# A two-layer hybrid decoder step: prompt memory in quarters between the mixers' products, the SSD norm behind the GLA chunks, and two more output tiles in halves

## The chip, the cores and the metric

One core of a Trainium2 chip. The metric is the device time of one execution in microseconds, the median of three runs for the kernel before. All data is fp32, so each matrix product appears in the trace as two MATMUL instructions.

## The reference

One inference step for a prompt group (256 tokens) and a sample group (8 sequences of 8 tokens) through two layers of width 1024. 320 token columns are processed together. Cut to what matters here:

```python
xn = rms_norm(x, norm_mix)
h = xn @ w_in                                     # split among the three mixers
o_mla = mla_attend(...)                           # 8 heads; samples over 16 cached pages of 128 tokens each
o_ssd = ssd_mixer(...)                            # Mamba-2 chunk scan, 4 heads, old state h0, then norm per group
o_gla = gla_mixer(...)                            # gated linear attention, chunks of 64, old state S0, then norm
x = x + concat([o_mla, o_ssd, o_gla]) @ w_o
x = x + mem_attend(rms_norm(x, norm_mem), mk, mv) # prompt: mk, mv from mem_prompt (256 tokens); samples: cached
x = x + conv_ffn(rms_norm(x, norm_ffn))

def mem_kv(mem, lp):
    k = rms_norm((mem @ mem_wk).reshape(b, n, MEM_HEADS, MEM_HEAD_DIM), mem_k_norm)
    v = (mem @ mem_wv).reshape(b, n, MEM_HEADS, MEM_HEAD_DIM)
```

The updated states of SSD and GLA, the latents, mk and mv are outputs too.

## The kernel before, in words

Activations lie with their features on the 128 partitions: x is 8 key tiles of 320 columns (256 prompt columns TP, then 64 sample columns). Each engine has its own program, written out by hand in the order in which it runs; they meet in semaphores. A PSUM bank is taken from a named ring (`proj`: banks 0 to 2, `score`: 3 and 4, `mix`: 5 to 7) by `banks.open`, filled by TensorE (`banks.full`), and given back by the engine that empties it; the next opener waits for that (`banks.before`).

Per layer, TensorE's program is: 18 tiles of the input projection with the latent attention's inputs between them; `memory_keys(l, 0)`; `prompt_attention`; `tokens_first` (transposes of values and convolved inputs to tokens); `gla_decay`; `ssd`; `gla_inputs`; `ssd_norm`; `gla`; `gla_norm`; `cache` (the samples' attention over 128 pages, 32 groups of four); `mixed_out`; `memory`; `mlp`.

**Prompt memory.** `memory_keys(l, part, some)` makes a tile of 128x256: parts 0 and 1 are the two key tiles mk, 2 and 3 the two value tiles mv, 4 the sum of squares of mk. `some` is the range of key tiles k of this call, and a tile may be spread over calls. Before, parts 1 to 3 run in halves of four key tiles (L1015) in the attention's iterations h = 1 to 6. ScalarE copies the finished tiles in its own attention loop, at h = 2, 4, 6 and 7 (L2152 and the copies at L1863).

**SSD.** TensorE's `ssd` makes cumulative sums (L695, L696, L706), decays (L713), C·B products (L719), the chunk states h1 and h2 (L729 to L736), then for each group g the interaction with old states `yi` (L745, and sixteen narrow products at L748, which read hT, the old SSD state transposed) and the products `y` (L759). VectorE puts Y together (L1453 to L1466), ScalarE squares it, TensorE sums the squares (`y_ss`, L778), ScalarE makes the factor of it (L1868, L1871), and VectorE's `ssd_out` (L1472) writes mix tiles 4 and 5. ScalarE in `ssd` also scales the old state in its natural layout, hnat, in sixteen copies (L1863, after a wait for hnat_in), and only then empties GLA's key transposes (`kwt`) in five copies, also L1863 (`gla_keys`).

**GLA.** `gla_inputs` transposes keys (L794, L795) and makes the scores (L800). TensorE's `gla` begins with a wait for `kwt` to be emptied, then runs four chunks c: state increments (L810), a product for the new SSD state (`ssd_states`, L769), outputs (L821, L824); then the samples (L833, L838), the samples' state (L847), the last `ssd_states`, and in `gla_norm` the sums of squares (`o_ss`, L858). The cache's first product (L877) follows.

**Output projection.** For tiles m = 0 to 2 (`EARLY` = 3) the prompt's columns are done during the end of `cache` (`mixed_out_prompt`, L969). `mixed_out` then waits for the last sample's attention, makes `ov_new` (L977, L978), and runs eight tiles at L992: m = 0 to 2 over the 64 sample columns only, m = 3 to 7 over all 320. Each has eight key tiles, in `MIX_ORDER` (4, 5, 6, 7, 0, 1, 2, 3). VectorE adds each tile to x in `residual` (L1625), in the order of m.

**Weights and states.** Weights come through a ring of seven slots of 512 KB, in the order of `SLOTS`, on SyncE's DMA queue. `fill` (L2460) waits, slot by slot, until the last reader of what the slot held has signalled: for the two tiles of memory input and the two of wv that reader is value tile 1 (`"mv", l, 1`). Around the mixers SyncE's program is in this order:

```python
sp.dma_start(hT_t, io["ssd_t"][l]).then_inc(hT_in, 16)        # L2500
limit[:] = [filled[0] + NSLOT]
fill(("wuv", "wo"))                                           # L2460: wuv, then wo tiles 0 to 5
...
sp.dma_start(hnat_t, io["ssd_n"][l]).then_inc(hnat_in, 16)    # L2506
...
sp.dma_start(gsb_t, io["gla"][l]).then_inc(gsb_in, 16)        # L2509
for t in range(2):
    group(l, t)                                               # L2468, L2479: cache pages
sp.wait_ge(*on["mix_gla"].at(l, 1))
```

Slots that wo tiles 0 and 1 take held the memory input, tiles 2 and 3 take wk's, and 4 and 5 take wv's.

Of the kernel before, what the change touches and what calls it, by code (L numbers as in the profile page):

```python
# [27 lines left out]
ACT = mybir.ActivationFunctionType  # L28
# [178 lines left out]
def trunk(nc, io):  # L207
    ctx = ExitStack()
    with ctx:
# [285 lines left out]
        def _(pe):  # L495
# [151 lines left out]
            def prompt_attention(l):  # L647
                for h in range(HEADS + 3):
                    if h < HEADS:
                        prompt_scores(l, h)  # L650
                    if 1 <= h <= 6:
                        memory_keys(l, (h + 1) // 2, range(0, 4) if h % 2 else range(4, KD))
                    if h == 7:
                        memory_keys(l, 4)
                    if 0 <= h - 2 < HEADS:
                        prompt_values(l, h - 2)
                    if h >= 3:
                        prompt_out(l, h - 3)

            def gates(l):  # L660
# [7 lines left out]
                last.then_inc(banks.full("gate", l), 1)  # L668

            def tokens_first(l):  # L670

                for f in (4, 5):
                    b = banks.open("mix", "tok", l, f)
                    pe.wait_ge(*banks.before("tok", l, f))
                    for i in range(2):
                        pe.transpose(b[:, i * P:(i + 1) * P], gv[:, f - 4, i * P:(i + 1) * P], cc("ident"))
                    pe.transpose(b[0:TS, 2 * P:3 * P], gv[:, f - 4, TP:T], cc("ident")).then_inc(banks.full("tok", l, f), 1)
                pe.wait_ge(*on["xu_ready"].at(l))
                for f in range(4):
                    b = banks.open("mix", "tok", l, f)  # L680
                    pe.wait_ge(*banks.before("tok", l, f))
                    for i in range(2):
                        pe.transpose(b[:, i * P:(i + 1) * P], xu[:, f, i * P:(i + 1) * P], cc("ident"))
                    pe.transpose(b[0:TS, 2 * P:3 * P], xu[:, f, TP:T], cc("ident")).then_inc(banks.full("tok", l, f), 1)
# [4 lines left out]
            def ssd(l):  # L689
# [51 lines left out]
                pe.wait_ge(hT_in, 16 * (l + 1))  # L741
                for g in range(2):
                    b = banks.open("mix", "yi", l, g)
                    pe.wait_ge(*banks.before("yi", l, g))
                    mm(b[:, P:TP], h1[:, g, :], xu[:, 4 + g, P:TP], **F)  # L745
                    for s in range(NB):
                        at = TP + NQ * s
                        last = mm(b[:, at:at + NQ], hT[:, g, s, :], xu[:, 4 + g, at:at + NQ], **F)  # L748
                    last.then_inc(banks.full("yi", l, g), 1)
                for g in range(2):  # L750
                    b = banks.open("mix", "y", l, g)
                    pe.wait_ge(*banks.before("y", l, g))
                    for i in range(3):
                        n = P if i < 2 else TS
                        pe.wait_ge(*banks.emptied("G", l, i))
                        pe.wait_ge(*on["xdt_ready"].at(l))
                        for hh in range(2):
                            h = 2 * g + hh
                            last = mm(b[64 * hh:64 * hh + 64, i * P:i * P + n], tok[0:n, i, h * 64:h * 64 + 64],  # L759
                                      dec[0:n, i, h, 0:n], **F)  # L760
                    last.then_inc(banks.full("y", l, g), 1)
# [40 lines left out]
            def gla(l):  # L802
# [32 lines left out]
                for s in range(NB):  # L835
                    for hh in range(2):
                        out = b[64 * hh:64 * hh + 64, 0:P].rearrange("p (g t) -> p g t", g=2)[:, :, NQ * s:NQ * s + NQ]
                        last = mm(out, gsb[:, s, :], qtm[:, hh::2, TP + NQ * s:TP + NQ * s + NQ],  # L838
                                  start=False, stop=(s == NB - 1))
                last.then_inc(banks.full("o", l, 4), 1)  # L840
                pe.wait_ge(*on["vm_ready"].at(l))
                for half in range(2):
# [9 lines left out]
            def gla_norm(l):  # L852

                pe.wait_ge(*on["o_sq"].at(l))
                for g in range(2):
                    b = banks.open("mix", "o_ss", l, g)
                    pe.wait_ge(*banks.before("o_ss", l, g))
                    mm(b[:, 0:T], cc("blk64"), sq[:, g, :], **F).then_inc(banks.full("o_ss", l, g), 1)  # L858

# [111 lines left out]
            def mixed_out(l):  # L971

                pe.wait_ge(*banks.emptied("po", l, NB - 1))
                b = banks.open("mix", "ov_new", l)
# [5 lines left out]
                last.then_inc(banks.full("ov_new", l), 1)  # L980
                for m in range(KD):
                    split = m < EARLY
                    if split:
                        w, b, at = early[m], banks.of("wo", l, m), TP
                    else:
                        w, at = slot("wo", m, "wo", l, m).rearrange("p (k c) -> p k c", k=KD), 0
                        b = banks.open("proj", "wo", l, m)
                        pe.wait_ge(*banks.before("wo", l, m))
                    for k in MIX_ORDER:
                        if m == 0 and k == 0:  # L990
                            pe.wait_ge(*banks.emptied("ov_new", l))
                        last = mm(b[:, at:T], w[:, k, :], mix[:, k, at:T], start=(k == MIX_ORDER[0]), stop=(k == MIX_ORDER[-1]))  # L992
                    last.then_inc(banks.full("wo", l, m), 1)

            mem_slots = []
# [192 lines left out]
            for l in range(DEPTH):  # L1188
# [25 lines left out]
                gla_inputs(l)  # L1214
                ssd_norm(l)
                gla(l)
# [8 lines left out]
        def _(dve):  # L1225
# [283 lines left out]
            def gla(l):  # L1509
                for c in range(4):  # L1510
# [11 lines left out]
                    dve.wait_ge(*V.last)  # L1522
                ssd_out(l)
                dve.wait_ge(gsb_in, 16 * (l + 1))
                TTO(gso, gsb, ge[:, TP + NQ - 1:T:NQ].unsqueeze(2).broadcast_to([P, NB, 64]), ALU.mult).then_inc(V.step(), 1)
                dve.wait_ge(*V.last)
                for half in range(2):
# [3 lines left out]
                    TTO(o, o, b[:, 0:256].rearrange("p (b v) -> p b v", b=4), ALU.add).then_inc(V.free("dSs", l, half), 1)  # L1531
                states(l, 1, 1)
                dve.wait_ge(*on["o_rs"].at(l))
                for g in range(2):
# [322 lines left out]
        def _(act):  # L1857
# [129 lines left out]
            def prompt_attention(l):  # L1987
                scale = QK ** -0.5
                for h in range(HEADS + 3):
# [14 lines left out]
                    if h == 2:  # L2004
                        zg_sigmoid(l, 1)
                    if h in (2, 4, 6, 7):
                        memory_keys(l, (h + 1) // 2)

# [14 lines left out]
            def ssd(l):  # L2023
# [4 lines left out]
                for k in range(4):  # L2028
                    token_tile(l, k)
                gla_decay(l)  # L2030
                act.wait_ge(*on["cs_diff"].at(l))
# [12 lines left out]
                act.wait_ge(*on["g_diff"].at(l))  # L2044
                exp(gek, gek, scale=1.0 / 16).then_inc(A.fire(on["gek_ready"]), 1)
                own_samples(l, bm, 256, "bm_ready")
                act.wait_ge(hnat_in, 16 * (l + 1))
# [7 lines left out]
                f(sq[:, 0:2, :], ysb, ACT.Square).then_inc(A.fire(on["y_sq"]), 1)  # L2055
                for g in range(2):
                    b = banks.of("y_ss", l, g)
                    act.wait_ge(*banks.filled("y_ss", l, g))
                    ln(ytmp[:, g, :], b[:, 0:T], 128).then_inc(A.free("y_ss", l, g), 1)
                act.wait_ge(*A.last)  # L2060
                exp(ytmp, ytmp, scale=-0.5).then_inc(A.fire(on["y_rs"]), 1)

# [16 lines left out]
            def gla(l):  # L2079
# [4 lines left out]
                act.wait_ge(*A.last)  # L2084
                f(sq[:, 0:2, :], osb, ACT.Square).then_inc(A.fire(on["o_sq"]), 1)
                for g in range(2):
# [651 lines left out]
```

## Time and profile before

| | |
|---|---|
| runs, median (lowest to highest) | 1406.98 us (1404.48 to 1411.47) |
| profiled execution, its own time | 1413.27 us |
| its span, first to last instruction | 1411.5 us |
| mean granted TensorE clock | 0.976 of full speed |
| TensorE busy | 1375.7 us (97%) |
| TensorE weight load busy | 1131.1 us (80%) |
| VectorE, ScalarE, GpSimd busy | 894.0, 594.0, 206.0 us |
| DMA | 175.24 MB, mean 124 GB/s |

Shares of busy time are averages over stages. Matmuls are pipelined, so a busy TensorE isn't one at its peak, and a product takes twice as long when the granted clock is 0.50 as when it is 1.00. An instruction's line can be that of a helper: L1863 is every ScalarE copy, L1871 every exponential.

### The profile page before, as it was taken

To read this page: it belongs to the slowest core of one execution; us is meant where nothing else is said; L and a number is where in the kernel's file an instruction comes from. 1 tells how busy PE (TensorE), PEld (TensorE's weight loads), DVE (VectorE), ACT (ScalarE), POOL (GpSimd) and SP (SyncE) were. 2 spreads that over 40 slices of the span, in tenths; PEclk is the share of its full clock that TensorE was granted. 3 is DMA by queue.
4 is the path that set the end of the run, shared out by engine and by line. 5 is a ranking of instruction groups with operands and counts; after the bars stand their busy time and mean duration, and the time that the engine had idled before them with its cause. 6 is when DMAs were issued, how large, how long until landed. Compare 5 with 4: busy or idle time off the path is not lost.

```text
span 1411.5 us, 23318 instructions
## 1 busy us (share of the span) xinstructions
PE 1375.7 (97%) x8148; PEld 1131.1 (80%) x8148; DVE 894.0 (63%) x1850; ACT 594.0 (42%) x1607; POOL 206.0 (15%) x330
## 2 busy tenths in 40 slices
PE   8999899999998999999999999999999999999999
PEld 6676767777775899999976677677778669999999
DVE  1337658888325878797423565688882258878964
ACT  2166647767215333320012766577761253333200
POOL 1001112221011222220000101211200121222200
PEclk9999989999989999999999998999998999999999
DMA  7331434443034344444433323444421353444442
GB/s 272 111 121 60 168 104 130 124 112 96 21 128 170 120 150 134 136 136 144 141 133 123 106 93 121 129 129 114 123 69 60 105 185 120 150 127 143 132 137 88
DMA packets 79718, 175.24 MB, mean 124 GB/s; under 512 B 11793, under 2 KB 46130, under 8 KB 78706
## 3 DMA queue, kind: packets, MB, share of 16 engines
q1 hardware_dynamic: 75952, 164.11, 36.5%
q0 software_dynamic: 3360, 9.18, 2.1%
q8 instruction: 66, 1.08, 0.3%
q14 instruction: 50, 0.41, 0.1%
q10 hardware_dynamic: 290, 0.45, 0.1%
HBM read 167.42 MB, written 6.29 MB: 123 GB/s over the span
## 4 chain that ended last, share of the span: by engine, by line
PE 62%; DVE 25%; ACT 9%; issue 3%; DMA 1%; SPq 1%; DVEq 0%
PE pair L517 13%; PE pair L877 8%; DVE area L1675 8%; PE pair L878 8%; PE pair L1149 8%; PE pair L992 5%; ACT area L1871 4%; PE bank L1149 3%; PE bank L913 2%; DVE area L1693 2%; DVE area L1699 2%; PE pair L884 2%; ACT area L1877 2%; PE pair L969 2%; DVE area L1691 2%
## 5 line engine op out<-in xcount | busy, mean ns | idle before, releaser
L517 PE MATMUL pair<-xg,slot 128*128 128x320 f32 x768 | 212.2, 434 | 3.0 <-DMA slot<-in_weights 2.2
L1544 DVE TENSOR_REDUCE small<-sq 128x8 f32<-128x512 f32 x256 | 168.1, 682 | 47.2 <-ACT sq L2110 45.4
L517 PEld LDWEIGHTS pair<-xg,slot 128*128 128x128 f32 x768 | 144.9, 190 | 65.9 <-issue 2.9
L2110 ACT ACTIVATE sq<-pair 128x512 f32<-128x512 f32 x256 | 152.3, 595 | 5.8 <-DVE small L1544 5.8
L1675 DVE TENSOR_TENSOR area<-slot 128x512 f32<-128x512 f32 (+1 forms) x128 | 85.4, 668 | 42.7 <-PE pair L1149 42.7
L1118 PE MATMUL pair<-sq,area 128*128 128x160 f32 x736 | 112.1, 301 | 0.1
L877 PE MATMUL pair<-wkq,area 128*128 128x288 f32 x320 | 107.6, 418 | 0.0
L1118 PEld LDWEIGHTS pair<-sq,area 128*128 128x128 f32 x736 | 102.8, 190 | 1.9 <-DVE area L1675 1.2
L878 PE MATMUL pair<-wkq,area 128*128 128x288 f32 x320 | 103.8, 406 | 0.0
L1871 ACT ACTIVATE area<-area 128x336 f32<-128x336 f32 (+6 forms) x114 | 62.1, 549 | 94.1 <-DVE area L1693 79.9
L2315 POOL DMA_INDIRECT krT<-in_cache_r,kr_rows x64 | 61.2, 956 | 223.8 <-PE pair L884 221.4
L1863 ACT ACTIVATE xg<-pair 128x64 f32<-128x64 f32 x256 | 56.1, 219 | 84.0 <-PE pair L878 53.2
L2223 ACT ACTIVATE area<-area,par 128x336 f32<-128x336 f32 x44 | 29.4, 668 | 142.3 <-DVE area L1716 141.1
L1863 ACT ACTIVATE area<-pair 128x160 f32<-128x160 f32 (+6 forms) x156 | 45.2, 309 | 97.4 <-PE pair L1149 91.6
L1863 ACT ACTIVATE area<-bank 128x160 f32<-128x160 f32 (+8 forms) x112 | 39.4, 364 | 85.5 <-PE bank L1149 57.6
L1118 PE MATMUL pair<-olat,slot 128*128 128x160 f32 x480 | 75.0, 299 | 0.0
L878 PEld LDWEIGHTS pair<-wkq,area 128*128 128x128 f32 x320 | 60.8, 190 | 16.8
L877 PEld LDWEIGHTS pair<-wkq,area 128*128 128x128 f32 x320 | 56.2, 190 | 17.6 <-issue 1.4
L1118 PEld LDWEIGHTS pair<-olat,slot 128*128 128x128 f32 x480 | 68.6, 190 | 0.3
L2307 POOL TENSOR_SCALAR xg<-x,par 128x320 f32<-128x320 f32 x24 | 29.4, 1227 | 261.5 <-DVE x L1625 181.1
L992 PE MATMUL pair<-mix,slot 128*128 128x320 f32 (+1 forms) x256 | 67.4, 443 | 0.0
L877 PE MATMUL pair<-wkq,kept 128*128 128x288 f32 x192 | 65.5, 423 | 0.4 <-DMA kept<-in_cache 0.2
(456 smaller groups left out, 2700.9 us busy)
## 6 DMA issues: line engine op xcount, KB each, us to landing
slot<-in_weights SPq DMA_DIRECT2D x216, 512.0 KB, 3.6
area<-in_cache SPq DMA_DIRECT2D x160, 130.0 KB, 2.1
kept<-in_cache SPq DMA_DIRECT2D x96, 130.0 KB, 2.2
slot<-in_weights SPq DMA_DIRECT2D x18, 384.0 KB, 3.6
xg<-in_ssd_t SPq DMA_DIRECT2D x2, 1024.0 KB, 4.7
area<-in_ssd_n SPq DMA_DIRECT2D x2, 1024.0 KB, 11.6
hs_out<-area POOLq DMA_DIRECT2D x2, 1024.0 KB
x<-in_x SPq DMA_DIRECT2D x4, 320.0 KB, 6.4
```

What stands on the lines that cost most here:

```text
L517: last = mm(out[:, 0:T], w[:, k, :], xg[:, k, :], start=(k == 0), stop=(k == KD - 1))
L877: mm(pair[:, 0:288], page, wkq[:, 0:4, at:at + 72], **F)
L878: last = mm(pair[:, 512:800], page, wkq[:, 4:8, at:at + 72], **F)
L992: last = mm(b[:, at:T], w[:, k, :], mix[:, k, at:T], start=(k == MIX_ORDER[0]), stop=(k == MIX_ORDER[-1]))
L1118: last = mm(out[:, 0:HALF], held[:, k, :], moving[:, k, :], start=(k == 0), stop=(k == 3))
L1149: last = mm(out[:, 0:HALF], held[:, k, :], moving[:, at + k, :], start=(b == 0 and k == 0), stop=(b == 2 and k == n - 1))
L1544: dve.tensor_reduce(ssk[:, t % 2, 8 * j:8 * j + 8], ksq[k % 3], AX.X, ALU.add).then_inc(V.fire(on["k_summed"]), 1)
L1675: TTO(w[k], a, b, op).then_inc(V.fire(on["w_sum"]), 1)
L1863: return f(out, in_, ACT.Copy, **kw)
L1871: return f(out, in_, ACT.Exp, **kw)
L2110: f(ksq[k % 3].rearrange("p (a h) d -> p a h d", a=2), b4[:, :, :, NQ - at:NQ - at + 64], ACT.Square).then_inc(A.fire(on["key_free"]), 1)
L2315: pool.indirect_dma_start(out=krT[n % KR_GROUPS][:, :], out_offset=None, in_=io["cache_r"].rearrange("l a c t -> (l a c) t"), in_offset=ba ...
```

## The change

TensorE's prompt attention keeps parts 1 (in quarters, h = 1 to 4), 4 and half of part 2; the rest of part 2 goes among the token transposes, and part 3 in two halves around the second `yi` group. ScalarE's copies of these tiles move along. `ssd_norm` goes from ahead of `gla` to behind the samples' outputs in it; ScalarE's factor for Y goes behind the GLA outputs, with GLA's squares in other tiles of sq; VectorE's `ssd_out` goes behind the last state. In the output projection, tiles 3 and 4 are made in halves of four key tiles, and the order of tiles is changed. SyncE's and GpSimd's programs are not edited.

```diff
@@ -648,10 +648,12 @@
                         prompt_scores(l, h)
-                    if 1 <= h <= 6:
-                        memory_keys(l, (h + 1) // 2, range(0, 4) if h % 2 else range(4, KD))
+                    if 1 <= h <= 4:
+                        memory_keys(l, 1, quarter(h - 1))
                     if h == 7:
                         memory_keys(l, 4)
+                    if h in (8, 9):
+                        memory_keys(l, 2, quarter(h - 8))
                     if 0 <= h - 2 < HEADS:
@@ -666,6 +668,9 @@
                 last.then_inc(banks.full("gate", l), 1)
+
+            def quarter(i):
+                return range(2 * i, 2 * i + 2)
@@ -677,6 +682,8 @@
                 for f in range(4):
+                    if f >= 2:
+                        memory_keys(l, 2, quarter(f))
                     b = banks.open("mix", "tok", l, f)
@@ -740,6 +747,8 @@
                 for g in range(2):
+                    if g:
+                        memory_keys(l, 3, range(0, 4))
                     b = banks.open("mix", "yi", l, g)
@@ -747,6 +756,7 @@
                     last.then_inc(banks.full("yi", l, g), 1)
+                memory_keys(l, 3, range(4, KD))
                 for g in range(2):
@@ -838,6 +848,7 @@
                 last.then_inc(banks.full("o", l, 4), 1)
+                ssd_norm(l)
                 pe.wait_ge(*on["vm_ready"].at(l))
@@ -855,7 +866,7 @@
                     pe.wait_ge(*banks.before("o_ss", l, g))
-                    mm(b[:, 0:T], cc("blk64"), sq[:, g, :], **F).then_inc(banks.full("o_ss", l, g), 1)
+                    mm(b[:, 0:T], cc("blk64"), sq[:, 2 + g, :], **F).then_inc(banks.full("o_ss", l, g), 1)
@@ -970,6 +981,7 @@
+                first_half(l, 3)
                 pe.wait_ge(*banks.emptied("po", l, NB - 1))
@@ -978,19 +990,28 @@
                 last.then_inc(banks.full("ov_new", l), 1)
-                for m in range(KD):
-                    split = m < EARLY
-                    if split:
-                        w, b, at = early[m], banks.of("wo", l, m), TP
+                first_half(l, 4)
+                for m in (0, 3, 1, 4, 2, 5, 6, 7):
+                    split, half = m < EARLY, m in (3, 4)
+                    if split or half:
+                        w, b, at = early[m], banks.of("wo", l, m), TP if split else 0
                     else:
...
                         pe.wait_ge(*banks.before("wo", l, m))
-                    for k in MIX_ORDER:
+                    for k in MIX_ORDER[4:] if half else MIX_ORDER:
                         if m == 0 and k == 0:
...
                     last.then_inc(banks.full("wo", l, m), 1)
+
+            def first_half(l, m):
+
+                early[m] = slot("wo", m, "wo", l, m).rearrange("p (k c) -> p k c", k=KD)
+                b = banks.open("score", "wo", l, m)
+                pe.wait_ge(*banks.before("wo", l, m))
+                for k in MIX_ORDER[:4]:
+                    mm(b[:, 0:T], early[m][:, k, :], mix[:, k, :], start=(k == MIX_ORDER[0]), stop=False)
@@ -1212,7 +1233,6 @@
                 gla_inputs(l)
-                ssd_norm(l)
                 gla(l)
@@ -1520,7 +1540,6 @@
                     dve.wait_ge(*V.last)
-                ssd_out(l)
                 dve.wait_ge(gsb_in, 16 * (l + 1))
@@ -1530,6 +1549,7 @@
                 states(l, 1, 1)
+                ssd_out(l)
                 dve.wait_ge(*on["o_rs"].at(l))
@@ -2003,8 +2023,10 @@
                         zg_sigmoid(l, 1)
-                    if h in (2, 4, 6, 7):
-                        memory_keys(l, (h + 1) // 2)
+                    if h == 5:
+                        memory_keys(l, 1)
+                    if h == 8:
+                        memory_keys(l, 4)
@@ -2027,6 +2049,7 @@
                     token_tile(l, k)
+                memory_keys(l, 2)
                 gla_decay(l)
@@ -2043,6 +2066,7 @@
                 exp(gek, gek, scale=1.0 / 16).then_inc(A.fire(on["gek_ready"]), 1)
+                memory_keys(l, 3)
                 own_samples(l, bm, 256, "bm_ready")
@@ -2053,12 +2077,6 @@
                 f(sq[:, 0:2, :], ysb, ACT.Square).then_inc(A.fire(on["y_sq"]), 1)
-                for g in range(2):
-                    b = banks.of("y_ss", l, g)
-                    act.wait_ge(*banks.filled("y_ss", l, g))
-                    ln(ytmp[:, g, :], b[:, 0:T], 128).then_inc(A.free("y_ss", l, g), 1)
-                act.wait_ge(*A.last)
-                exp(ytmp, ytmp, scale=-0.5).then_inc(A.fire(on["y_rs"]), 1)
@@ -2082,7 +2100,13 @@
                 act.wait_ge(*A.last)
-                f(sq[:, 0:2, :], osb, ACT.Square).then_inc(A.fire(on["o_sq"]), 1)
+                f(sq[:, 2:4, :], osb, ACT.Square).then_inc(A.fire(on["o_sq"]), 1)
+                for g in range(2):
+                    b = banks.of("y_ss", l, g)
+                    act.wait_ge(*banks.filled("y_ss", l, g))
+                    ln(ytmp[:, g, :], b[:, 0:T], 128).then_inc(A.free("y_ss", l, g), 1)
+                act.wait_ge(*A.last)
+                exp(ytmp, ytmp, scale=-0.5).then_inc(A.fire(on["y_rs"]), 1)
                 for g in range(2):
```

## Rows read from the trace of the kernel before

**Rows 1.** The page: busy time of TensorE, and engines' shares of the last chain.

```profile
PE 1375.7 (97%) x8148; PEld 1131.1 (80%) x8148; DVE 894.0 (63%) x1850; ACT 594.0 (42%) x1607; POOL 206.0 (15%) x330
...
PE 62%; DVE 25%; ACT 9%; issue 3%; DMA 1%; SPq 1%; DVEq 0%
```

**Rows 2.** Windows: stretch: length, busy by engine (instructions), PEclk, DMA share, GB/s.

```profile
120.00:150.00 30.00, 27.12 (x140) 21.65 (x140) 20.79 (x63) 21.46 (x65) 2.10 (x2) 1.00 0.23 84
150.00:167.00 17.00, 15.14 (x128) 13.86 (x126) 9.60 (x26) 11.48 (x33) 0.00 (x0) 1.00 0.50 189
167.00:178.00 11.00, 10.05 (x64) 6.24 (x64) 7.20 (x14) 7.68 (x25) 4.50 (x5) 0.69 0.12 36
178.00:194.00 16.00, 16.00 (x137) 8.36 (x134) 6.17 (x13) 3.61 (x10) 1.69 (x3) 0.61 0.09 36
...
849.00:866.00 17.00, 15.14 (x100) 13.89 (x98) 7.33 (x18) 8.36 (x27) 0.00 (x0) 0.80 0.47 175
...
363.00:380.00 17.00, 16.70 (x127) 14.23 (x127) 2.74 (x7) 1.67 (x3) 0.00 (x0) 1.00 0.00 1
380.00:396.00 16.00, 15.13 (x70) 14.09 (x71) 2.65 (x6) 2.24 (x5) 2.35 (x2) 0.59 0.40 131
```

**Rows 3.** Timeline of SyncE's queue: start us, length us, instruction; both layers.

```profile
145.12 0.47 SPq L2506 DMA_DIRECT2D area<-in_ssd_n  x1
...
844.06 0.48 SPq L2506 DMA_DIRECT2D area<-in_ssd_n  x1
```

**Rows 4.** Waits of SyncE's queue, 110 to 200 us: in total, times, longest.

```profile
SPq L2460 <- PE pair L1015: 26.4, 1, 26.4
```

**Rows 5.** DMA of the SSD state: issue to landing in layer 0, and both layers.

```profile
area<-in_ssd_n SPq DMA_DIRECT2D x1, 1024.0 KB, 12.1
...
DMA to landing us min/median/max: 11.0/11.6/12.1
```

**Rows 6.** Timeline of TensorE, layer 0: start us, us, instruction, [idle before].

```profile
140.32 1.89 PE L1015 MATMUL pair<-slot 128*128 128x256 f32 x8
...
166.38 2.14 PE L748 MATMUL bank<-mix,xg 128*128 128x8 f32 x16
...
176.23 1.34 PE L778 MATMUL bank<-sq,const 128*128 128x320 f32 x4
177.51 0.32 PE L810 MATMUL pair<-area,kept 128*32 128x64 f32 x8
...
182.36 0.44 PE L810 MATMUL pair<-area,kept 128*32 128x64 f32 x8
...
185.78 0.69 PE L833 MATMUL bank<-area 64*64 64x64 f32 x8
...
193.56 1.17 PE L877 MATMUL pair<-wkq,kept 128*128 128x288 f32 x2
```

**Rows 7.** Timeline of ScalarE, layer 0.

```profile
133.53 0.36 ACT L2152 ACTIVATE sq<-pair 128x256 f32<-128x256 f32 x1
...
167.03 4.76 ACT L1863 ACTIVATE area<-area 128x128 f32<-128x128 f32 x16
173.33 1.45 ACT L1863 ACTIVATE kept<-pair 64x128 f32<-64x128 f32 x5 [1.54 <-PE pair L795]
```

**Rows 8.** Timeline of TensorE, layer 1.

```profile
839.01 1.89 PE L1015 MATMUL pair<-slot 128*128 128x256 f32 x8
...
868.32 1.85 PE L748 MATMUL bank<-mix,xg 128*128 128x8 f32 x16
...
879.87 0.32 PE L810 MATMUL pair<-area,kept 128*32 128x64 f32 x8
...
892.70 1.17 PE L877 MATMUL pair<-wkq,kept 128*128 128x288 f32 x2
```

**Rows 9.** Timeline of TensorE, layer 0, output projection.

```profile
380.87 0.43 PE L977 MATMUL bank<-olat,slot 128*128 128x64 f32 x2 [0.98 <-DVE olat L1586]
```

## The prediction

> **What bounds the kernel now.** The page comes first: TensorE is busy 97% of the span and carries 62% of the chain that ended last [rows 1], so the two questions are where it works at half clock and where it has nothing to do. The windows by stage answer both [rows 2]. The prompt attention (120 to 150 us) has 2.9 us of gaps at full clock; the state space mixer's start has 1.9 us; from 167 to 178 the granted clock is 0.69 and from 178 to 194 it is 0.61; the output projection's start, 380 to 396, has 0.59. The two levels are 1.2 and 2.4 GHz, so 0.59 over 16 us means 13.1 us at 1.2 GHz. Layer 1 repeats the pattern some 699 us later. These are the places that the change fills with dense matmuls. The third view is SyncE's queue with its waits and landings [rows 3, 4, 5]. The weight slots of the output projection are reloaded into the slots of the memory input, and those count as read when the second tile of prompt memory values is full. SyncE waited 26.4 us for that, at L2460, and only behind those six loads does it issue the natural-layout SSD state (145.12), the GLA state and the first pages.
>
> **The change, part by part, against the profiled execution** (1413.27 us; its span is 1411.5). That execution is 6.3 us above the median of 1406.98; a difference from it carries over to the median.
>
> *Memory quarters out of the attention.* Four key tiles of matmuls take 1.73 us (1.89 with the tail, [rows 6]). The attention loses three such halves, 5.2 us of TensorE, and keeps three. Per head it is then ScalarE's and VectorE's chain that sets the pace. What ScalarE saves on it is the key tile's square and copy between two heads' exponentials, 133.53 to 134.06 [rows 7], 0.53 us, and that at h = 7 a little less stands ahead of the last heads; I take 0.6 (ends 0 and 1.2). The two quarters among the token transposes fit into the 1.9 us of gaps of 150 to 167 [rows 2]: nothing, and if that cover were gone, 0.85 us each.
>
> *Memory halves around the interactions with the old state.* Two halves, 3.5 us, now stand before and behind the second group (L748), whose last matmul ended at 166.38 + 2.14 = 168.5 [rows 6]. So the second value tile is full at 168.5 + 3.5 - 0.6 = 171.4, and at about 170.9 if the denser stretch also keeps the clock up through L748. It was full at 140.32 + 1.89 = 142.2. In layer 1 the old end is 870.2. That layer lies 3.2 us further behind layer 0 there than at its start, after the stretch 849 to 866 at clock 0.80 [rows 2, 8]; the quarters should keep that clock up, which gives 870.2 + 3.5 - 0.6 - 3.2 = 869.9, against 840.9 before.
>
> *What is queued behind that.* SyncE waits for this tile before six slot loads (3 MB) and then 1 MB of SSD state. From tile full to state landed took 145.12 + 12.1 - 142.2 = 15.0 us in layer 0 and 844.06 + 11.0 - 840.9 = 14.2 us in layer 1 [rows 3, 5, 6, 8]. ScalarE used that state at 167.03, 9.8 us after it landed; this cover is gone. It now lands at 170.9 + 15.0 = 185.9 and at 869.9 + 14.2 = 884.1. ScalarE reaches the wait early (it now also waits for the value tile, and copies the samples' B rows in 1.7 us), scales the state in 4.76 us and copies the GLA key tiles in 1.45 us [rows 7], and without those TensorE may not start the GLA chunks (L810). They start at 192.1 and 890.3 where they started at 177.51 and 879.87: 14.6 and 10.4 us later. In the meantime TensorE has its Y products and GLA scores and then nothing, for about 13 us. The y_ss product (1.34 us with its tail) goes from ahead of the chunks to behind them; all that work, and VectorE's, lies in the wait.
>
> *From the chunks to the cache.* It took 193.56 - 177.51 = 16.05 us in layer 0, mostly at 1.2 GHz, and 892.70 - 879.87 = 12.83 us in layer 1, mostly at 2.4 [rows 6, 8]. Now y_ss comes on top. Upper bound, all at 1.2 GHz: 1.0 for the first chunk, three turns like 182.36 to 185.78 (10.3), 7.8 for the rest (to 193.56), twice y_ss's 1.07 (2.1): 21.2. Lower bound, clock as in layer 1: 12.83 + 1.3 = 14.1. Behind a long gap the nearest row is layer 0's second half, where this same mix stayed at the low level once there; I take 20 in both layers: +3.9 and +7.2. Sum for the mixers: 14.6 + 3.9 + 10.4 + 7.2 = **+36.1 us**. ssd_out's two instructions on VectorE (1.0 us) go to where it idled 3 us for ScalarE: nothing.
>
> *Output projection.* A dense first half of tile 3 (four key tiles of 320 columns, 2.1 us) covers the 0.98 us that TensorE waited at 380.87 [rows 9]; tile 4's covers ScalarE's copy; the second halves stand between the narrow passes. Dense halves of 2.1 us then alternate with 1.8 us of narrow ones. At 363 to 380 [rows 2], 3.7 us dense against 2.1 us narrower, the clock was 1.00. If it stays up here too, 13.1 us at half clock become 6.5. I count 6.6 + 1.0 = 7.6 per layer, **-15.2 us**; lower bound 2 (the gaps alone). The slots of tiles 3 and 4 are of the early batch; the later tiles' slots (wuv's and tile 0's) are freed within about 2 us of before and read over 12 us later: nothing. No DMA is added. VectorE's residual takes tiles in their old order and gets tile 1 later than tile 3; the last tile is still last: nothing.
>
> Sum: 36.1 - 15.2 = +20.9, so 1434 for the profiled execution and **1427 us** for the median.
>
> Two rules of the Trainium skill weigh on this. The trace first: the state landed 15.0 and 14.2 us after the release, its 4.2 MB sharing with some 1.3 MB of pages and GLA state behind it. "DMA: Bandwidth & Descriptors" (Bandwidth) gives 425 GB/s for large transfers, by which 4.2 MB would be an estimated 10 us, and the sum about 10 us lower. The second is among the rivals.
>
> **The rivals.**
> A, *the memory release doesn't hold the state back*. It ends faster. The place is SyncE's order, the price the 25 us of late chunk starts. If the state landed within 2 us of the release, the chunks would start about where they did: 1407 - 15.2 for the projection - 3.2 for layer 1's stretch + 2 for the Y products behind the memory halves, some 1390. It decides at the landing: with 20 us from chunks to cache the change breaks even at about 4 us from release to landing, with 14 at about 10. The wait row, with its releaser L1015, speaks against it [rows 4], and so do both landings. 5%.
> B, *short wait and warm chunks*: the transfer needs only what its own 4.2 MB take at the 390 GB/s or so of the old burst (11 us), and the GLA chunks climb to full clock as in layer 1: -7.2 -11.8 from my sum, 1408. Between it and the forecast lie the cases where one of the two holds. For it: layer 1's chunks ran warm. Against: they came straight from 4 us of dense scores, these come from nothing. 14%.
> C, *the projection stays at half clock*: half of the mixture is still narrow; only the gaps are won, +13.2, so 1440. Against: 363 to 380. 12%.
> D, *the attention goes cold*: rid of three dense halves, its heads keep a third of transposes. In layer 1, 849 to 866 fell to 0.80 right behind a run of transposes and gaps, and lost 3.2 us. The same in each attention gives +6.4 to the value tile and all behind it: 1433. "TensorE: Matmul & The Clock Gate" (Part 4) says that transposes don't count as work for the clock; by that rule the attention would fall in both layers, and the trace agrees as far as layer 1. 11%.
> E, *the edit doesn't do what it says*: y_ss and the quarters change nothing by themselves. It ends in one of the above.
>
> **How the numbers follow.** Forecast 58%, A 5%, B 14%, C 12%, D 11%. The range takes B's upper part, D and C: 1412 to 1441. A measurement can tell about 0.5%, 7 us. Faster by more than that: A, 5%. Within it, 1400 to 1414: B's lower half and the lowest end of the forecast, 9%. Slower: 86%.
>
> **What would show it.** SyncE's wait at L2460 grows from 26 to 55 us; ScalarE has a wait of some 13 us before its sixteen state copies, TensorE one of about the same before L810; DMA is busy at 171 to 186, not 142 to 158. The chunks run at clock 0.5 to 0.7. The projection's first 16 us show a clock near 1.0 and no gap ahead of L977. I am wrong if the copies start at 167 to 173 as before, or if the release is signalled from inside the attention.

## The result and the profile after

The changed kernel takes 1440.08 us (median of 4 executions, 1438.1 to 1443.02) beside 1405.73 us for the kernel before. The ratio is 1.022, with a 95% interval of 1.0177 to 1.0263: slower by 25 to 37 us. Forecast were 1427 us and a range of 1412 to 1441. The profiled execution took 1438.1 us, which is 24.8 us more than that of before (1413.27); the sum in the prediction was made against that one and gave 20.9.

The windows of the kernel after, by stage (columns as in [rows 2], which they answer to). The third to fifth are the wait, the chunks of layer 0 and the projection; the last three lie in layer 1:

```profile
120.00:150.00 30.00, 24.89 (x118) 18.30 (x117) 20.79 (x63) 20.86 (x64) 2.10 (x2) 0.94 0.00 1
150.00:167.00 17.00, 16.76 (x131) 15.19 (x131) 10.12 (x26) 9.69 (x29) 0.00 (x0) 1.00 0.01 2
178.00:194.00 16.00, 2.81 (x26) 1.41 (x26) 0.50 (x2) 6.93 (x23) 0.00 (x0) 0.59 0.62 232
194.00:212.00 18.00, 18.00 (x122) 8.93 (x122) 5.50 (x11) 3.77 (x9) 1.61 (x3) 0.50 0.05 17
...
404.00:428.00 24.00, 24.00 (x119) 18.51 (x118) 6.02 (x13) 4.64 (x10) 5.60 (x5) 1.00 0.52 174
...
862.00:879.00 17.00, 16.76 (x131) 15.19 (x131) 9.91 (x26) 9.69 (x29) 0.00 (x0) 1.00 0.01 3
...
890.00:903.00 13.00, 0.00 (x0) 0.00 (x0) 0.00 (x0) 5.85 (x21) 0.00 (x0) 0.53 0.77 290
903.00:925.00 22.00, 21.77 (x149) 10.97 (x150) 6.19 (x13) 5.29 (x13) 1.70 (x3) 0.50 0.05 20
```

The reader sees three things. The stretch behind the attention, which fell to 0.80 in layer 1 before, is at 1.00 in both layers. The projection, at 0.59 before, is at 1.00. Between them TensorE does nothing at all for 13 us (no instruction from 890 to 903, while DMA runs at 290 GB/s), and all the work from the chunks to the cache then runs at 0.50, the lower of the clock's two levels.

Why it stands still is told by SyncE's queue in the kernel after: its wait between 110 and 200 us, the issues in layer 0, and (DMA view, 140 to 220 us) the landing of the state there. They answer to [rows 3 to 5]:

```profile
SPq L2484 <- PE pair L1036: 55.9, 1, 55.9
```

```profile
171.30 2.84 SPq L2484 DMA_DIRECT2D slot<-in_weights  x6
174.23 0.44 SPq L2530 DMA_DIRECT2D area<-in_ssd_n  x1
```

```profile
area<-in_ssd_n SPq DMA_DIRECT2D x1, 1024.0 KB, 10.8
```

The wait for the second value tile (L1036 is the old L1015) has grown from 26.4 to 55.9 us; the state that stood at 145.12 in the queue is issued at 174.23. On the other side ScalarE, layer 0, answers to [rows 7]:

```profile
171.30 0.38 ACT L1883 ACTIVATE mv<-pair 128x256 f32<-128x256 f32 x1 [6.44 <-PE pair L1036]
171.72 1.71 ACT L1883 ACTIVATE area<-area,const 64x256 f32<-64x256 f32 x4
185.02 4.78 ACT L1883 ACTIVATE area<-area 128x128 f32<-128x128 f32 x16 [11.59 <-DMA area<-in_ssd_n]
189.70 1.44 ACT L1883 ACTIVATE kept<-pair 64x128 f32<-64x128 f32 x5
```

And TensorE, layer 0 and then the first chunk and the cache of layer 1, to [rows 6, 8, 9]; L820 is the chunks' first product (old L810), L888 the cache's (old L877), L1014 a first half of tiles 3 and 4:

```profile
169.29 1.97 PE L1036 MATMUL pair<-slot 128*128 128x256 f32 x8
...
191.19 0.44 PE L820 MATMUL pair<-area,kept 128*32 128x64 f32 x8 [15.46 <-ACT kept L1883]
...
212.68 1.17 PE L888 MATMUL pair<-wkq,kept 128*128 128x288 f32 x2
...
398.68 2.37 PE L1014 MATMUL pair<-mix,slot 128*128 128x320 f32 x8
...
427.42 4.47 PE L517 MATMUL pair<-xg,slot 128*128 128x320 f32 x16
...
903.23 0.44 PE L820 MATMUL pair<-area,kept 128*32 128x64 f32 x8 [15.28 <-ACT kept L1883]
...
924.71 1.17 PE L888 MATMUL pair<-wkq,kept 128*128 128x288 f32 x2
```

The row at 427.42 is the memory stage's first product. In the kernel before it stood here (TensorE, layer 0):

```profile
416.23 4.47 PE L517 MATMUL pair<-xg,slot 128*128 128x320 f32 x16
```

Taken from these rows and their old counterparts, the 24.8 us are:

| where | layer 0 | layer 1 |
|---|---|---|
| chunks start later | +13.7 | +10.4 |
| chunks to cache | 21.5 instead of 16.05: +5.4 | 21.5 instead of 12.8: +8.7 |
| from the cache's start to the memory's first product behind the projection | -7.9 | -7.1 |

That is 38.2 - 15.0; the remaining 1.6 lies between the layers, where layer 1's attention starts 13.0 us later than before and layer 0's memory stage 11.2. There the 64 us from the memory's first product on ran at a granted clock of 0.97, against 1.00 before; why isn't known. (In the table, 13.0 is taken off the times of layer 1.)

### The profile page after: what moved, and what is told of

The parts are those of the page before. It is cut to its first block, busy times and chain, and to the rows that moved or that the text cites. A ratio compares the mean times of both kernels' runs of the same rounds, so it can differ in the third digit from the quotient of the medians.

```text
span 1436.3 us, 23318 instructions
## 1 busy us (share of the span) xinstructions
PE 1372.7 (96%) x8148; PEld 1121.1 (78%) x8148; DVE 892.7 (62%) x1850; ACT 594.9 (41%) x1607; POOL 207.0 (14%) x330
## 4 chain that ended last, share of the span: by engine, by line
PE 62%; DVE 23%; ACT 9%; issue 3%; DMA 2%; SPq 1%; DVEq 0%
PE pair L517 12%; PE pair L888 9%; PE pair L889 8%; DVE area L1695 8%; PE pair L1170 7%; ACT area L1891 4%; PE pair L1005 3%; PE bank L1170 2%; PE bank L924 2%; DVE area L1713 2%; ACT area L1883 2%; PE pair L895 2%; DVE area L1719 2%; ACT area L1897 2%; PE pair L980 2%
## 5 line engine op out<-in xcount | busy, mean ns | idle before, releaser
L888 PE MATMUL pair<-wkq,area 128*128 128x288 f32 x320 | 107.6, 418 | 0.0
L1883 ACT ACTIVATE area<-pair 128x160 f32<-128x160 f32 (+8 forms) x154 | 44.8, 309 | 98.2 <-PE pair L1170 91.6
L888 PEld LDWEIGHTS pair<-wkq,area 128*128 128x128 f32 x320 | 56.2, 190 | 17.6 <-ACT sq L2134 1.4
L888 PE MATMUL pair<-wkq,kept 128*128 128x288 f32 x192 | 66.1, 426 | 0.0
L889 PE MATMUL pair<-wkq,kept 128*128 128x288 f32 x192 | 63.6, 414 | 0.0
```

Source lines behind the costliest of these rows:

```text
L888: mm(pair[:, 0:288], page, wkq[:, 0:4, at:at + 72], **F)
L889: last = mm(pair[:, 512:800], page, wkq[:, 4:8, at:at + 72], **F)
L1883: return f(out, in_, ACT.Copy, **kw)
```

## The experiments

Two theories. **The release**: everything that was lost comes from SyncE's order, in which the state stands behind the slots that the second value tile frees. The rival, **the mixture**: the matmuls moved in among the mixers, or the sum of squares behind the chunks, cost time by themselves, on TensorE's path or through its clock. The third question, apart from both, is what the projection gives. Ratios are to the kernel before, on the same chip in the same series, with the 95% interval.

**The changed kernel, with the states issued first.**

```diff
                 sp.dma_start(hT_t, io["ssd_t"][l]).then_inc(hT_in, 16)
-                limit[:] = [filled[0] + NSLOT]
-                fill(("wuv", "wo"))
-                limit.clear()
...
                 for t in range(2):
                     group(l, t)
+                limit[:] = [filled[0] + NSLOT]
+                fill(("wuv", "wo"))
+                limit.clear()
```

The fill now stands behind the loads of both states and the first two groups of pages. Expected:

> The changed kernel, with SyncE issuing the natural-layout SSD state, the GLA state and the first eight pages ahead of the seven weight slots. Theory (the whole loss is the state that lands 14 to 15 us after a release that now comes 29 us later): ScalarE's sixteen copies start right behind the samples' B rows, at about 173.4 us in layer 0, the GLA chunks at about 179.5 instead of 191.2, and the chunks take 16 to 18 us instead of 21.5. That is some 16 us less per layer, and about 22 us less in each with the clock's share at best: 1390 to 1405 us, below the kernel before by up to 1%. Rival (the memory halves between the products with the old state and the norm behind the chunks cost by themselves, by their time and their clock): the chunks start earlier but the time stays at 1420 us or more, ratio above 1.01.

Measured: 1415.09 us, ratio 1.004 (1.0017 to 1.0062), 12 executions. Most of the loss is gone, yet it falls short of what the release theory expected. The state was issued at 115.1 us and took this long to land (DMA view, 110 to 190 us):

```profile
area<-in_ssd_n SPq DMA_DIRECT2D x1, 1024.0 KB, 6.8
```

So it was there at 122, and still the chunks began late. ScalarE and TensorE in layer 0 of this run, and the windows from the chunks to the cache in both layers:

```profile
171.41 0.38 ACT L1883 ACTIVATE mv<-pair 128x256 f32<-128x256 f32 x1 [6.44 <-PE pair L1036]
171.83 1.71 ACT L1883 ACTIVATE area<-area,const 64x256 f32<-64x256 f32 x4
173.44 4.77 ACT L1883 ACTIVATE area<-area 128x128 f32<-128x128 f32 x16
178.11 1.44 ACT L1883 ACTIVATE kept<-pair 64x128 f32<-64x128 f32 x5
```

```profile
179.60 0.32 PE L820 MATMUL pair<-area,kept 128*32 128x64 f32 x8 [3.75 <-ACT kept L1883]
```

```profile
179.00:201.00 22.00, 21.40 (x150) 10.78 (x151) 6.18 (x13) 6.07 (x14) 1.70 (x3) 0.54 0.19 74
878.00:900.00 22.00, 21.37 (x148) 10.69 (x149) 6.18 (x13) 5.61 (x13) 1.70 (x3) 0.50 0.15 59
```

A second wait had been hidden behind the first. The change put the copy of value tile 1 ahead of the state's scaling in ScalarE's program; it waits 6.44 us for TensorE, and the GLA key copies, for which the chunks wait, come 3.75 us too late. Behind a gap of 3.75 us the chunks run at half clock, in layer 1 from their first product on as behind a gap of 15.5. In layer 0 they begin at full clock (their first row takes 0.32 us, against 0.44) and fall within the first 4 us.

**The kernel before, with the states issued first.** The same edit of SyncE's order, and nothing else.

> The kernel before, with the same new order on SyncE. Theory: the state was there 9.8 us before its use and the output projection's weights are read 200 us later, so nothing moves: ratio 0.997 to 1.003. Rival (the burst of weights and states itself slowed something in the attention, so that any new order gains): 5 us or more below the kernel before, and then the first run restores nothing.

Measured: 1406.37 us, ratio 0.9985 (0.9957 to 1.0013). Nothing: in the kernel before the state's landing was hidden, as [rows 7] against [rows 3, 5] say.

**The kernel before, with the release made late.** No matmul is moved; SyncE just waits, ahead of the fill, for the products that now stand beside the second value tile.

```diff
+                sp.wait_ge(*banks.filled("yi", l, 1))
                 limit[:] = [filled[0] + NSLOT]
                 fill(("wuv", "wo"))
```

> The kernel before, TensorE, ScalarE and VectorE as they were; SyncE alone also waits, before the seven slot loads, for the second group of products with the old state (full at 168.5 us in layer 0, 870.2 in layer 1). Theory: the state lands about 14 us after that, at 182.5, the GLA chunks start at about 188.8 instead of 177.5 and take 19 instead of 16 us; in layer 1 10 us later and 6 longer. Together 28 to 32 us: 1434 to 1438 us, though not one matmul has moved. Rival (the loss is in the moved matmuls): 1403 to 1409 us.

Measured: 1444.54 us, ratio 1.0239 (1.0174 to 1.0303). Timeline of SyncE's queue, ScalarE and TensorE of this run, layer 0, and its chunks in layer 1 (L778 is `y_ss`, L810 the chunks' first product, as in [rows 6]):

```profile
168.35 3.32 SPq L2460 DMA_DIRECT2D slot<-in_weights  x7
171.78 0.67 SPq L2507 DMA_DIRECT2D area<-in_ssd_n  x1
...
184.61 4.78 ACT L1863 ACTIVATE area<-area 128x128 f32<-128x128 f32 x16 [17.72 <-DMA area<-in_ssd_n]
...
191.41 2.50 PE L778 MATMUL bank<-sq,const 128*128 128x320 f32 x4 [15.38 <-ACT sq L2055]
```

```profile
909.00:928.00 19.00, 19.00 (x145) 9.51 (x145) 6.27 (x13) 3.80 (x9) 1.70 (x3) 0.50 0.04 16
```

The wait alone, with the memory's matmuls and the sum of squares where they always were, makes a gap of 15.38 us in layer 0 and 14.55 in layer 1, chunks at a clock of 0.60 and 0.50, and the kernel slower by 25 to 43 us; 1434 to 1438 us had been expected. A loss as large as the changed kernel's net one can thus be made without the mixture. The fair measure is the changed kernel with the old projection, further down (1.0328, its interval from 1.0267): by the ratios the late release makes some 34 of its 46 us, and the two intervals barely overlap. The profiled executions lie closer, 1450.58 us here and 1448.71 there. The release also comes 3 us earlier here (SyncE issues the fill at 168.35, in the changed kernel at 171.30). (Here `y_ss` is what waits, since ScalarE's squares stand behind the state's scaling; in the changed kernel it is the chunks.)

**The kernel before, with the new output projection.** `mixed_out` and `first_half` of the changed kernel, all else as before.

> The kernel before with the new mixed_out alone: first halves of tiles 3 and 4 ahead of and behind the samples' value products, second halves between the narrow passes. Theory: the gap of 1.0 us is covered and the granted clock stays at 1.00 through the narrow passes, 7.6 us per layer: 15.2 us, 1390 to 1392 us, ratio 0.989. Rival (the clock falls all the same when the stretch before it isn't the changed one): only the gaps, 2 us, ratio 0.998.

Measured: 1396.89 us, ratio 0.9909 (0.9873 to 0.9944): a gain of 8 to 18 us, 12.8 in the middle. The time is 5 us above the expected 1390 to 1392; the expected ratio, 0.989, lies in the interval.

**The changed kernel, states first, and ScalarE's copy moved behind the state's scaling.**

```diff
-                memory_keys(l, 3)
                 own_samples(l, bm, 256, "bm_ready")
...
+                memory_keys(l, 3)
                 gla_keys(l)
```

> The run with the states first, and ScalarE's copy of the second value tile moved from ahead of the samples' B rows to behind the sixteen state copies. There ScalarE had waited 6.4 us for that tile (until 171.3), so that GLA's key copies came 3.75 us after TensorE had run dry. Theory (that wait, with the gap and the clock it costs, is what the states-first run still lost): the chunks start at about 176 in layer 0, no gap ahead of them, and take 14 to 15 us; 1385 to 1393 us. Rival (the chunks fall to 1.2 GHz because the norm's dense product no longer stands ahead of them): they start at 176 but take 19 to 21 us, 1396 to 1406 us.

Measured: 1394.94 us, ratio 0.9921 (0.9893 to 0.9949), 2 us above the upper end of what was expected. The gap is gone and with it the half clock. TensorE's chunks of layer 0, and the windows from the chunks to the cache in both layers:

```profile
175.83 0.32 PE L820 MATMUL pair<-area,kept 128*32 128x64 f32 x8
```

```profile
176.00:188.00 12.00, 12.00 (x150) 6.53 (x143) 6.54 (x15) 4.33 (x12) 1.48 (x3) 1.00 0.51 192
864.00:876.00 12.00, 12.00 (x150) 6.41 (x149) 6.53 (x15) 4.32 (x11) 1.16 (x2) 1.00 0.53 198
```

The same 150 matmuls that took 21.5 us take 11.9. What is late next is seen at the cache's ninth pages, TensorE in both layers of this run:

```profile
198.94 0.75 PE L888 MATMUL pair<-wkq,kept 128*128 128x288 f32 x2 [2.27 <-DMA kept<-in_cache]
...
887.66 1.14 PE L888 MATMUL pair<-wkq,kept 128*128 128x288 f32 x2 [2.57 <-DMA kept<-in_cache]
889.55 1.17 PE L888 MATMUL pair<-wkq,kept 128*128 128x288 f32 x2
```

SyncE issues those pages only when the GLA output is done, and the faster chunks reach them sooner. From the cache's first product to the projection's first half it took 187.3 and 189.3 us here, 186.0 and 186.7 in the changed kernel: of the 9.6 us that the chunks gave in each layer, 1.3 and 2.6 went back. Issuing those pages earlier wasn't tried. Such waits aren't a matter of the memory's parts: in the version below that has these back in the attention, with chunks as fast, they are 2.18 and 2.55 us.

**The same, with the sum of squares of Y back ahead of the chunks.** `ssd_norm` between `gla_inputs` and `gla`, its factor and `ssd_out` in their old places.

> The same, and the norm of Y back ahead of the chunks on TensorE, ScalarE and VectorE. Theory of the wait: the norm's place is worth nothing either way, within 4 us of the run before this one. Theory of the norm: the chunks take 13 us again and this one is the faster by 10 to 14 us, 1383 to 1393.

Measured: 1393.41 us, ratio 0.9922 (0.9891 to 0.9954). Its place is worth nothing that can be measured in the time, either way. In the traces the chunks' clock differs: with the sum of squares among them and no gap ahead they were at 1.00 in all four cases (both layers of the run before this one and of the run with the memory's parts back). With it ahead of them and no gap they were at 1.00 from first to last in only two of ten; layer 1 of this run is one that fell, to 0.80 over 13.1 us. Whether its place is the cause wasn't tested by itself.

**The changed kernel, with only ScalarE's copy moved back.** As above, without the change of SyncE's order.

> The changed kernel with ScalarE's copy behind the state copies, SyncE's order untouched. The state lands at 185 whatever ScalarE does before that, so within 4 us of the changed kernel: 1434 to 1444. Rival (ScalarE's wait for the value tile is itself the loss): below 1425.

Measured: 1441.58 us, ratio 1.0252 (1.0194 to 1.031). No gain while the state is late: ScalarE waits at the state instead. This timeline row of its layer 0 shows the longer wait:

```profile
187.97 4.78 ACT L1883 ACTIVATE area<-area 128x128 f32<-128x128 f32 x16 [19.52 <-DMA area<-in_ssd_n]
```

The copy's wait costs something measurable only where the wait for the state is gone.

**The changed kernel, with the old output projection.**

> The changed kernel with the old mixed_out. From the prediction 15 us slower than the changed kernel, from the run with the new projection alone (13 us better than before) 13: 1452 to 1456 us, ratio 1.031 to 1.035. Rival (the projection's gain depends on the rest): 1445 or less.

Measured: 1450.05 us, ratio 1.0328 (1.0267 to 1.0388). The new projection gives some 10 us here by the medians and 15 by the ratios (1.0328 against 1.022), with wide intervals. The mixers' programs are those of the changed kernel, and yet in layer 0 the chunks behind a gap of 15.60 us took 19.4 us and not 21.5, since the clock rose just ahead of the cache. TensorE, layer 0 of this run:

```profile
193.16 0.44 PE L820 MATMUL pair<-area,kept 128*32 128x64 f32 x8 [15.60 <-ACT kept L1873]
...
212.53 0.65 PE L888 MATMUL pair<-wkq,kept 128*128 128x288 f32 x2
```

**The changed kernel, with the memory's matmuls and copies back in the attention.** The direct undo of that part (TensorE's and ScalarE's); SyncE's order, the place of the sum of squares and the projection stay as in the changed kernel.

```diff
-                    if 1 <= h <= 4:
-                        memory_keys(l, 1, quarter(h - 1))
+                    if 1 <= h <= 6:
+                        memory_keys(l, (h + 1) // 2, range(0, 4) if h % 2 else range(4, KD))
...
-                    if h in (8, 9):
-                        memory_keys(l, 2, quarter(h - 8))
...
```

> After, with the prompt memory's matmuls and copies back in the attention as before; the weights' issue, the norm of Y behind the chunks and the new projection stay as in after. The SyncE theory: the slot of value tile 1 is free at about 142 us again, the state is issued by about 146 and lands by about 158, the chunks start at 173 to 178 in layer 0 and the kernel takes 1390 to 1400 us (before, less what the new projection gave by itself, 12.8 us). The rival, by which the norm of Y behind the chunks or its factor in ScalarE's later place costs something of its own once the state is early: chunks to cache over 17 us and a time of 1403 or more.

Measured: 1399.38 us, ratio 0.9929 (0.9902 to 0.9955), at the upper end of what the release theory said. SyncE's queue issues the state where it did before, and TensorE's chunks of layer 0 (now L813) start without a wait. They start at 181.82, not at 173 to 178 as expected; the 17 us from 154.82 on ran at a granted clock of 0.70 here, and the 10 us behind them at 0.52. But the windows from the chunks to the cache, with the sum of squares still among them, are at full clock or nearly so in both layers:

```profile
144.81 0.39 SPq L2519 DMA_DIRECT2D area<-in_ssd_n  x1
```

```profile
181.82 0.32 PE L813 MATMUL pair<-area,kept 128*32 128x64 f32 x8
```

```profile
181.00:194.00 13.00, 13.00 (x153) 6.99 (x153) 6.90 (x15) 4.33 (x11) 1.49 (x3) 0.98 0.03 11
872.00:885.00 13.00, 13.00 (x154) 7.12 (x153) 6.93 (x15) 4.82 (x12) 1.70 (x3) 1.00 0.09 29
```

**The kernel before, with the states first and the new projection.**

> Before, with the states and first pages issued ahead of the weights and the new projection; the memory's matmuls in the attention as in before. If the projection is the whole of the gain, this ties with the version that has the memory's parts in the mixers, the states first and the copy behind them (0.9921): ratio 0.988 to 0.994. If that redistribution has a gain of its own (chunks that ran at full clock throughout there), this one is at 0.995 or more and its chunks show a granted clock under 0.9. If the redistribution cost something of its own (the cache's wait for pages there, 2.3 and 2.6 us, with the stretches at half clock behind it), this one is under 0.988, and its cache groups wait for no page.

Measured: 1401.0 us, ratio 0.9936 (0.9911 to 0.9961). It ties with the version that keeps the memory's parts in the mixers (0.9921). Its window ahead of the chunks of layer 1, and then the same window of the run with states first and the copy moved, where the parts are in the mixers (there it takes in the first 2 us of the chunks):

```profile
850.00:866.00 16.00, 15.76 (x108) 14.91 (x109) 12.29 (x28) 9.36 (x26) 1.37 (x2) 0.71 0.03 10
```

```profile
850.00:866.00 16.00, 15.76 (x127) 11.88 (x127) 12.46 (x28) 11.13 (x32) 4.46 (x5) 1.00 0.36 120
```

The redistribution does keep the clock up (1.00 in the second, 0.71 in the first), as meant. Over all the profiled kernels, the first 16.5 us behind the attention ran at 0.69 to 0.79 in five of twelve cases with the parts in the attention, and at 1.00 in all twelve with the parts in the mixers. Yet the end isn't earlier by anything measurable. The page waits take some of it back, but this version has one too, 2.50 us in layer 0 (none in layer 1), so they account for little of the tie; where the rest went stays open. Of the versions tried none beats the simplest, the kernel before with the new projection alone (0.9909); the four others that have the new projection and an early state (0.9921 to 0.9936) tie with it.

## Why the prediction was right

**The release: right, nearly to the microsecond.** Value tile 1 was full at 169.29 + 1.97 = 171.3 (said: 170.9). In layer 1 the tile was full at 883.5 against a forecast of 869.9 without layer 0's delay, of which 13.0 us had come by then: 870.5. SyncE waited 55.9 us (said: 55), ScalarE 11.59 ahead of the sixteen copies (said: 13). The run with nothing but a late release shows that this wait makes most of such a loss by itself. The runs with states first and the copy moved, and with the memory's parts back in the attention, show that the parts' new place and the sum of squares cost nothing measurable once the state is early. Only ScalarE's copy does (below).

**From tile full to state landed: 13.8 and 13.5 us**, for the 15.0 and 14.2 that I carried over from the kernel before. By the rule of the Trainium skill that I had set beside it, "DMA: Bandwidth & Descriptors" (Bandwidth), the estimate was 10 us; the measured values lie between, nearer to the trace.

**Start of the chunks: +13.7 and +10.4 us** for +14.6 and +10.4. TensorE's gap of 15.46 us was put at 13.

**Chunks to cache: mis-sized.** I took 20 us and kept 21.2 as the upper bound, for all at half clock; both layers took 21.5, all at half clock. This term is +14.1 instead of +11.1. The upper bound held the right clock and was 0.3 us short; the step that failed was to stay below it. It isn't a fixed cost: the run with the old projection took 19.4 us in layer 0 (0.56) and 21.5 in layer 1 with the same programs.

**Attention: -0.6 us was nothing.** From its first scores to the first token transpose it took 28.2 us in both layers after and 28.3 in both before. The pace is set elsewhere than by the two ScalarE instructions that left. Rival D, the cold attention, didn't come about either: the clock was 0.94 in layer 0 (it fell to 0.57 from 129 to 133 us, behind a wait of 1.88) and 1.00 in layer 1 (834 to 862), and the length the same. "TensorE: Matmul & The Clock Gate" (Part 4) of the Trainium skill says that transposes don't count as TensorE work in the same way, and the prediction took from it that the attention would fall in both layers. The trace doesn't bear that out for this stretch, in which 24 of 113 TensorE instructions (a third of the matrix products) are transposes beside dense scores.

**Projection: -15.2 said, -15.4 measured** in the profiles: 36.4 us to the memory's first product (with the gap ahead of L977) became 28.7 in each layer, from the row at 398.68 on. The gap ahead of L977 is covered and the clock is 1.00. In the medians of the run with this part alone it is 12.8 (8 to 18). Rival C is out.

**Rival A**, that the release doesn't hold the state, was false as to the kernel, but the time that it gave, 1390, is near what comes out when the release is undone and the copy doesn't wait: 1393 to 1399 in three versions. There the prediction had a blind spot. It said of ScalarE that it "now also waits for the value tile" and counted that at nothing, with the state's wait as the cover; it didn't say what it costs if that cover is gone. By the ratios of the two versions that differ in it alone, 1.004 - 0.9921, it cost some 17 us (about 12 to 22): gaps of 3.75 us and two mixers at half clock. That is why the first expectation of 1390 to 1405 was missed by ten.

**Sum.** +24.8 us between the profiled executions for +20.9: the start of the chunks is 0.9 lower, chunks to cache 3.0 higher, the last line of the table 0.2 higher, and 1.6 us came up between the layers. The medians lie further apart than the profiles, 34 us; the interval of the ratio is 25 to 37, with the profiles' difference at its lower end, and the profiled execution of before lay 6 to 8 us above its kernel's medians. The rest of that spread isn't explained. Part of this is luck: the median of 1440.08 is 13 us above the forecast and only 0.9 us inside the range, whose upper end was there for rivals C and D, and neither came about.

## What to carry to other kernels

Before you move a computation later, ask who else counts its end: a ring slot's last reader, and on the same DMA queue every load that merely stands behind that slot's refill. The cheap remedy is to issue loads with a free target ahead of those that wait for a release, and the same holds on an engine whose program puts a copy that can wait ahead of one that others wait for. And a gap of a few microseconds ahead of narrow matmuls can cost more than itself: 3.75 us here went with 9 to 10 us more in the chunks behind. Price the stretch behind such a gap at half clock.

## What the runs showed of the hardware

- How long the same 1 MB load takes from issue to landing goes with what stands ahead of it in its queue: 6.8 us with one other state load (1 MB) ahead, 10.4 to 12.1 us behind 3 MB of weights (the kernels after and before, both layers), 12.8 us behind 3.5 MB in the run with the late release.
- The chunks' mixture of narrow matmuls ran at either level with TensorE busy throughout, and changed level in its course. Behind waits of 15.46 and 15.28 us it was at 0.50 for all of its 21.5 us, behind 3.75 us at 0.50 to 0.54, and with no gap right ahead and the sum of squares among them the same instructions ran at 1.00 and took 11.9. I hadn't expected that 3.75 us would do nearly as much as 15. But a gap isn't needed for a fall: in [rows 6] a row of eight equal matmuls takes 0.32 us at 177.51 and 0.44 at 182.36, with no gap between. And the level can rise again: 0.56 over 19.4 us in layer 0 of the old projection. In layer 0 of the late release the chunks began at the low level and had 0.60 over 16.4 us (without the sum of squares among them).
- Dense halves of 2.1 us between narrow passes of about 1.8 us hold the full clock through 24 us of projection, where narrow passes in a row had 0.59.
